# First group's gate stage: SP issues the stores of combined weights between and behind the two halves of a step's second block of weights

## The chip, the cores and the metric

The kernel runs on one core of a Trainium2 chip. The metric is the device time of one execution in microseconds (us), the median of three runs.

## The reference

A two-layer decoder trunk over 2048 tokens of width 1024, all in float32. The first layer is a chunked gated MLP: RMS norm with adaLN shift and scale, one projection to `u`, `v` and `z` of width 2048 each, a layer norm of `v`, a causal mixing of 128 positions by a 128x128 matrix for each of 8 channel groups, and an output projection:

```
u, v, z = jnp.split(h @ w_in, 3, axis=-1)
u = jax.nn.gelu(u)
v = layer_norm(jax.nn.gelu(v), ln_g, ln_b)
mixed = jnp.einsum("gts,bnsgc->bntgc", ws, vc) + b_s.T[:, :, None]
y = u * mixed.reshape(B, S, A_WIDTH) * jax.nn.silu(z)
return y @ w_out
```

The second layer is sliding-window attention with a shared rotary K/V, and a final RMS norm follows. The change touches only how the first layer is scheduled.

## The kernel before

**Precision and units.** Every float32 weight is used as two parts, a rounded one and the rest: ACT copies `w_raw` to `w_hi` (rounding, L1364), POOL forms `w_lo` = `w_raw` - `w_hi` (L1130), and PE does three matmuls for each product (L2361 to L2363). PE's work is cut into units. A unit's weights are one block of 128x4x512, in two halves of 128x2x512 that are loaded, rounded and subtracted one by one.

**Groups, stages, steps.** The first layer runs over four groups of 512 tokens. In each group come first the `v` units, then the gate stage, then the output projection. The gate stage has eight steps, one for each channel group g. A step has a first block of weights (buffer `w_raw0`) and a second block (buffer `w_raw1`), 48 matmuls of 128x512 each, and then 16 small mixing matmuls (L2566, with `w_s`). PE takes the first block half by half, so that a half's buffer is free after half of the block; the second block's pieces alternate between the halves, so that both halves are free only when the block is done, that is when the mixing starts, and both are needed at the next second block's start.

**Combined weights.** Groups 2 to 4 compute `v` and the output projection with fewer products, out of sums and differences of weight blocks. Those combinations are made once, during the first group's gate stage, from weights loaded for it. The list `COMBS` has 16: eight for the output projection ("a" in the list, output combinations below) and eight for `v` ("v", V combinations). For one of them SP loads 1 MB into a place `cbr` (`load_comb`, L858), DVE forms it by three differences (L1946 128x1024, L1948 and L1950 128x512), ACT rounds it to `cbh` (L1388), POOL forms the rest `cbl` (L1149: one operation for an output combination, two for a V one), and SP stores it (`keep_comb`: an output one by three DMAs of 512 KB, L866 twice and L869; a V one by two of 1 MB, L866). There are four places; a load into a place waits until the place's last combination is stored (the wait stands in front of L858). Weights of the second layer are split in the same stage (`split`: ACT L1378, POOL L1140, stores L843 and L844).

**What sets the order.** Every engine's order is written out by hand. SP issues all of these DMAs from one queue, in program order, and stands still at each wait. Its program for a step is `a_stage(i, q)` with q = g + 4: it loads the two blocks of step g when their buffers come free, stores what `load_comb` fetched two stages earlier, and loads new combinations. For the first group, most stages have one output and one V combination; q = 11 stores two V combinations; q = 10 and 12 also store a split. POOL's order in a step is: rests of the first block, rests of the second, split, output combination, V combination. DVE's is: the gate's products for a group (L2071, L2074, L2078, L2084), then the two combinations.

Of the kernel before, what the change touches and what calls it, by code (L numbers as in the profile page):

```python
# [20 lines left out]
GROUPS = 8  # L21
# [23 lines left out]
FIRST_B = FIRST[NG]  # L45
# [15 lines left out]
def group_of(u):  # L61
    return max(i for i in range(NG) if FIRST[i] <= u)
# [6 lines left out]
def uz_unit(i, g, ku):  # L69
    return FIRST[i] + V_UNITS[i] + 2 * g + ku  # L70
# [34 lines left out]
def kept_split(u):  # L105

    return of_blocks(u) and factor_of(u)[0] == "T" and not kept_whole(u)
# [41 lines left out]
def pieces_in(u):  # L149
    return 4 if of_blocks(u) else 8  # L150
# [37 lines left out]
def buffers():  # L188


    taken, before, last, turn = [], [], {}, [0, 1]
    for u in range(UNITS):
        i = group_of(u) if u < FIRST_B else NG
        if product_of(u) is not None and (u - FIRST[i]) % 3 == 2:
            b = 2
        elif out_product_of(u) is not None and u - ao_first(i) >= 4 and (u - ao_first(i)) % 3 == 1:
            b = 2
        elif out_product_of(u) is not None and u - ao_first(i) == 1:
            b = 3
        else:  # L200
            b = turn.pop(0)
            turn.append(b)
        taken.append(b)
        before.append(last.get(b))
        last[b] = u
    return taken, before


BUFFER, BEFORE = buffers()


def by_halves(u):

    if of_blocks(u):
        return True
    if u < FIRST_B:
        return u % 2 == 0
    kind, g, n, ku = B_UNITS[u - FIRST_B]
    return kind == "kv" or ku == 0 or (kind == "b" and n == 1 and g < NG - 1) or (kind == "qz" and n == 3 and g == 0)


def freed(u, hh):

    half = pieces_in(u) // 2
    return half + half * hh if by_halves(u) else 2 * half
# [31 lines left out]
def combs_at(i, q):  # L257
    return [c for c, comb in enumerate(COMBS) if comb[0] == i and comb[1] == q]
# [136 lines left out]
def yoco_kernel(nc, x, c, positions, a_norm, a_ada_w, a_ada_b, a_w_in, a_ln_g, a_ln_b, a_w_s, a_b_s,  # L395
# [3 lines left out]
    with ctx:  # L399
# [176 lines left out]
        def sem(name, per_group=0):  # L576
            s = ctx.enter_context(nc.semaphore(name))
            per[name] = per_group
            return s
# [22 lines left out]
        piece_done, kv_full = sem("piece_done"), sem("kv_full", 1)  # L602
# [51 lines left out]
        def pieces(u, k):  # L654

            return PIECES_BY[u] + k
# [120 lines left out]
        def _(sp):  # L777
# [6 lines left out]
            def a_half(u, hh):  # L784
                p, i = BUFFER[u], group_of(u)
                n = u - FIRST[i]
                there = raw[p][:, 2 * hh:2 * hh + 2]
                if kept_split(u):
                    if product_of(u) is not None:
                        kept = cbd[product_of(u)[0], factor_of(u)[1], hh]  # L790
                    else:
                        kept = cad[factor_of(u)[1], out_product_of(u)[1], hh]
                    for part, w in ((0, whi[p]), (1, wlo[p])):
                        sp.dma_start(w[:, 2 * hh:2 * hh + 2].bitcast(F32), kept[part]) \
                            .then_inc(raw_in[2 * p + hh], 16)
                elif kept_whole(u):
                    sp.dma_start(there, cad[factor_of(u)[1], out_product_of(u)[1], hh, 0]) \
                        .then_inc(raw_in[2 * p + hh], 16)
                elif out_product_of(u) is not None:
                    (_, odd, cols_half), pair = factor_of(u), 4 * out_product_of(u)[1] + 2 * hh  # L800
                    sp.dma_start(there, wo2[:, pair:pair + 2, odd, 512 * cols_half:512 * cols_half + 512]) \
                        .then_inc(raw_in[2 * p + hh], 16)
                elif product_of(u) is not None:
                    sv, m = product_of(u)
                    _, rows_half, cols_half = FACTORS[m]
                    kt, col = 4 * rows_half + 2 * hh, WIDTH + 1024 * sv + 512 * cols_half
                    sp.dma_start(there, wa[:, kt:kt + 2, col:col + 512]).then_inc(raw_in[2 * p + hh], 16)
                elif n < V_UNITS[i]:
                    j, kt = n // 2, 4 * (n % 2) + 2 * hh
                    sp.dma_start(there, wa[:, kt:kt + 2, WIDTH + 512 * j:WIDTH + 512 * j + 512]) \  # L810
                        .then_inc(raw_in[2 * p + hh], 16)
                else:
                    g, kt = (u - uz_unit(i, 0, 0)) // 2, 4 * (n % 2) + 2 * hh
                    sp.dma_start(there[:, :, 0:GD], wa[:, kt:kt + 2, GD * g:GD * g + GD]) \
                        .then_inc(raw_in[2 * p + hh], 16)
                    sp.dma_start(there[:, :, GD:2 * GD], wa[:, kt:kt + 2, 2 * WIDTH + GD * g:2 * WIDTH + GD * g + GD]) \
                        .then_inc(raw_in[2 * p + hh], 16)

            def b_half(u, hh):
                p = BUFFER[u]  # L820
                for m, w in ((0, whi[p]), (1, wlo[p])):
                    sp.dma_start(w[:, 2 * hh:2 * hh + 2].bitcast(F32), wsd[split_of(u, hh), m]) \
                        .then_inc(raw_in[2 * p + hh], 16)
# [16 lines left out]
            def keep_split(s):  # L840
                sp.wait_ge(split_lo, s + 1)
                m = SPLIT_SLOT[s]
                sp.dma_start(wsd[s, 0], wsh[m][:].bitcast(F32)).then_inc(split_out[m], 16)  # L843
                sp.dma_start(wsd[s, 1], wsl[m][:].bitcast(F32)).then_inc(split_out[m], 16)  # L844
# [16 lines left out]
            def keep_comb(c):  # L861
                _, _, whose, n, m = COMBS[c]
                sp.wait_ge(comb_lo, c + 1)
                to, some = (cad[:, n // 4] if whose == "a" else cbd[n // 4]), rounded_combs(c)
                for part, w in ((0, cbh[m]), (1, cbl[m])):
                    sp.dma_start(to[some, n % 4 // 2, part, :, n % 2].rearrange("t p n -> p t n"),  # L866
                                 w[:, some].bitcast(F32)).then_inc(comb_out[m], 16)
                if whose == "a":
                    sp.dma_start(to[1:4:2, n % 4 // 2, 0, :, n % 2].rearrange("t p n -> p t n"), cbr[m][:, 1:4:2]) \  # L869
                        .then_inc(comb_out[m], 16)  # L870
# [5 lines left out]
            def a_stage(i, q):  # L876

                first = uz_unit(i, 0, 0) - 8
                if i == 0 and q == 12:

                    sp.wait_ge(comb_out[0], combs_out(0, 0))
                    sp.wait_ge(comb_out[1], comb_out_before(len(COMBS) - 1))
                if q >= 1:
                    unit(first + 2 * q)
                if q == GROUPS + 4:
                    unit(first + 2 * q + 1)
                s = split_at(i, q - 2)
                if s is not None:
                    keep_split(s)
                for c in combs_at(i, q - 2):  # L890
                    keep_comb(c)
                if 1 <= q < GROUPS + 4:
                    unit(first + 2 * q + 1)
                if i == 0 and q < 4:
                    for n in range(KT * (2 + q), KT * (3 + q)):
                        load_ada(n)
                for c in combs_at(i, q):
                    load_comb(c)
                s = split_at(i, q)
                if s is not None:  # L900
                    if i == 0:
                        sp.wait_ge(ada_used, 6 * KT)
                    load_split(s)

            def unit(u):
                if BUFFER[u] == 2:

                    sp.wait_ge(y_done, at("y_done", group_of(u) - (product_of(u) is not None), 8))
                elif BUFFER[u] == 3:

                    i = group_of(u)
                    sp.wait_ge(piece_done, PIECES_BY[uz_unit(i, 0, 0)])
                    sp.wait_ge(comb_out[0], combs_out(0, 0))
                for hh in range(2):
                    if BEFORE[u] is not None:
                        sp.wait_ge(piece_done, pieces(BEFORE[u], freed(BEFORE[u], hh)))
                    if u < FIRST_B:
                        a_half(u, hh)
                    else:
                        b_half(u, hh)  # L920

            def load_x(n):
                if n >= 1:
# [106 lines left out]
            for s, slot in enumerate(SLOTS):  # L1030
# [9 lines left out]
                for k, pc in enumerate(slot):  # L1040
                    u = FIRST_B + pc // 8
# [4 lines left out]
                    kind, ug, n, ku, q = unit_of(pc)  # L1046
# [18 lines left out]
                    kind, ug, n, ku, q = unit_of(pc - 5)  # L1065
# [1713 lines left out]
```

## Time and profile before

| | |
|---|---|
| median of 3 runs | 2218.93 us (2217.34 to 2219.06) |
| profiled execution, its own time | 2219.44 us |
| its span | 2217.7 us |
| busy: PE, DVE, ACT, POOL | 97%, 65%, 49%, 54% |
| DMA packets of SP's queue | 73.5% of 16 engines' span |
| first group's gate stage, from the first mixing to the last | 158.55 to 336.72 us |

The share of busy time is over the whole span. Where PE's next matmul starts late, the view of waits names the engine that it waited for. Register, semaphore and DMA-issuing instructions are not counted as busy; an operation that is held up after it has started is counted as busy for all that time.

### The profile page before, as it was taken

Reading aid. Unit: us, or ns where it says so; the run is one execution under the profiler, and the core shown is the slowest. Engines: PE = TensorE matmul, PEld = TensorE weight load, DVE = VectorE, ACT = ScalarE, POOL = GpSimd, SP = SyncE. Lnnn points to the kernel's source line nnn. Section 1 sums busy time; section 2 is a strip of 40 time slices with the busy share of each in tenths; the row PEclk is TensorE's granted clock in tenths of the full one; section 3 lists DMA queues with packets and bytes.
Section 4 is the critical chain, followed back from the end, with each engine's and each line's share of the span. In section 5 each row is a group of like instructions: output and inputs, shape, how many; then the busy total and the mean of one; then the engine's idle time right before and its main releaser. Section 6 shows DMA issues by size and latency. Waiting matters only on the chain.

```text
span 2217.7 us, 29383 instructions
## 1 busy us (share of the span) xinstructions
PE 2150.9 (97%) x10410; PEld 1801.0 (81%) x10410; DVE 1440.5 (65%) x1761; ACT 1095.3 (49%) x2050; POOL 1195.1 (54%) x913
## 2 busy tenths in 40 slices
PE   5999999999999999999999999999999999999998
PEld 4887778788888878888777888887888888888887
DVE  6956548757486864554974673767767657656854
ACT  4334446634545744445653445534545646545653
POOL 3456675845553865544594645441535555454542
PEclk9999999999999999999999999999999999999999
DMA  9888889785558785557877556899686697887654
GB/s 347 307 306 308 312 315 356 231 308 174 196 198 324 285 315 191 200 179 269 314 259 283 181 181 218 323 348 365 244 297 225 253 359 266 280 309 288 206 205 171
DMA packets 244787, 592.89 MB, mean 267 GB/s; under 512 B 20929, under 2 KB 96801, under 8 KB 244257
## 3 DMA queue, kind: packets, MB, share of 16 engines
q1 hardware_dynamic: 241680, 585.71, 73.5%
q10 hardware_dynamic: 2960, 5.30, 0.7%
q8 instruction: 83, 1.36, 0.2%
q14 instruction: 64, 0.52, 0.1%
HBM read 461.96 MB, written 119.54 MB: 262 GB/s over the span
## 4 chain that ended last, share of the span: by engine, by line
PE 75%; DMA 6%; POOL 6%; DVE 5%; ACT 3%; DVEq 2%; POOLq 1%; issue 1%; SPq 1%; ACTq 0%
PE ps L2361 22%; PE ps L2363 22%; PE ps L2362 22%; DMA w_raw<-in_a_w_in 3%; POOL w_lo L1130 3%; PE ps L2566 2%; PE ps L2615 1%; PE ps L2616 1%; POOL cbl L1149 1%; PE ps L2641 1%; DVE acc L1812 1%; ACT w_hi L1364 1%; DMA w_lo<-a_weights_combined 1%; PE ps L2650 1%; DVE yb L2093 1%
## 5 line engine op out<-in xcount | busy, mean ns | idle before, releaser
L1130 POOL TENSOR_TENSOR w_lo<-w_raw,w_hi 128x1024 fp32r<-128x1024 f32 x244 | 650.0, 2682 | 569.6 <-ACT w_hi L1364 569.4
L1364 ACT ACTIVATE w_hi<-w_raw 128x1024 fp32r<-128x1024 f32 x260 | 272.0, 1057 | 418.3 <-DMA w_raw<-in_a_w_in 372.7
L2361 PE MATMUL ps<-h,w_hi 128*128 128x512 f32 x1024 | 403.3, 394 | 9.7 <-POOL w_lo L1130 8.3
L2363 PE MATMUL ps<-h,w_lo 128*128 128x512 f32 x1024 | 398.9, 390 | 0.0
L2362 PE MATMUL ps<-h,w_hi 128*128 128x512 f32 x1024 | 398.7, 389 | 0.0
L2361 PEld LDWEIGHTS ps<-h,w_hi 128*128 128x128 f32 x1024 | 192.2, 188 | 55.3 <-POOL w_lo L1130 14.3
L2363 PEld LDWEIGHTS ps<-h,w_lo 128*128 128x128 f32 x1024 | 192.2, 188 | 40.7
L2362 PEld LDWEIGHTS ps<-h,w_hi 128*128 128x128 f32 x1024 | 192.4, 188 | 38.9 <-issue 0.2
L2361 PE MATMUL ps<-r,w_hi 128*128 128x512 f32 x480 | 191.6, 399 | 1.9 <-issue 1.9
L2363 PE MATMUL ps<-r,w_lo 128*128 128x512 f32 x480 | 187.7, 391 | 0.0
L2362 PE MATMUL ps<-r,w_hi 128*128 128x512 f32 x480 | 187.3, 390 | 0.0
L2361 PE MATMUL ps<-w_hi,yb 128*128 128x512 f32 x448 | 179.2, 400 | 7.1 <-DVE w_lo L2116 3.5
L2071 DVE SCALAR_TENSOR_TENSOR wz<-wz,ps 128x512 f32<-128x512 f32 x64 | 43.7, 686 | 210.5 <-ACT wz L1580 210.5
L2363 PE MATMUL ps<-w_hi,yb 128*128 128x512 f32 x448 | 175.8, 392 | 0.0
L2362 PE MATMUL ps<-w_lo,yb 128*128 128x512 f32 x448 | 175.6, 392 | 0.0
L2093 DVE TENSOR_TENSOR yb<-vy,yb 128x1024 fp32r<-128x1024 f32 x48 | 114.4, 2383 | 42.5 <-ACT yb L1540 39.2
L1269 POOL TENSOR_SCALAR_AFFINE_SELECT p_edge<-pt 64x256 fp32r<-64x256 f32 x64 | 27.1, 423 | 187.7 <-ACT pt L1735 186.5
L2361 PE MATMUL ps<-w_hi,r 128*128 128x512 f32 (+1 forms) x352 | 125.5, 357 | 2.7 <-DMA r<-kv_input 1.7
L1735 ACT ACTIVATE pt<-ps 128x512 fp32r<-128x512 f32 x64 | 38.4, 600 | 179.6 <-PE ps L2641 179.2
L2363 PE MATMUL ps<-w_hi,r 128*128 128x512 f32 (+1 forms) x352 | 123.6, 351 | 0.0
L2362 PE MATMUL ps<-w_lo,r 128*128 128x512 f32 (+1 forms) x352 | 123.5, 351 | 0.0
L2361 PE MATMUL ps<-w_hi,h 128*128 128x512 f32 x272 | 107.9, 397 | 4.5 <-POOL w_lo L1130 4.2
(277 smaller groups left out, 4902.6 us busy)
## 6 DMA issues: line engine op xcount, KB each, us to landing
w_raw<-in_a_w_in SPq DMA_DIRECT2D x256, 256.0 KB, 3.6
w_hi<-b_weights_split SPq DMA_DIRECT2D x104, 512.0 KB, 4.7
w_lo<-b_weights_split SPq DMA_DIRECT2D x104, 512.0 KB, 6.3
w_raw<-in_a_w_in SPq DMA_DIRECT2D x52, 512.0 KB, 4.7
w_raw<-in_a_w_out SPq DMA_DIRECT2D x48, 512.0 KB, 5.4
w_hi<-v_weights_combined SPq DMA_DIRECT2D x48, 512.0 KB, 3.9
w_lo<-v_weights_combined SPq DMA_DIRECT2D x48, 512.0 KB, 5.2
w_hi<-a_weights_combined SPq DMA_DIRECT2D x32, 512.0 KB, 6.6
```

The source lines that it names most:

```text
L1130: g.tensor_tensor(wlo[p][:, rows_], raw[p][:, rows_], whi[p][:, rows_].bitcast(F32), ALU.subtract).then_inc(w_lo, 1)
L1149: last = g.tensor_tensor(cbl[m][:, rows_], cbr[m][:, rows_], cbh[m][:, rows_].bitcast(F32), ALU.subtract)
L1269: return g.affine_select(out=heads, in_=in_, compare_op=ALU.is_ge, fill=0.0, base=0, pattern=[[0, 4], [1, HEAD]], channel_multiplier=-1)
L1364: s_.activation(whi[p][:, rows_], raw[p][:, rows_], ACT.Copy).then_inc(w_hi, 1)
L1735: s_.activation(pt[:, 0, :], bank(6), ACT.Copy).then_inc(pt_hi, 1)
L1812: v.scalar_tensor_tensor(there, rows_, sc[:, kt:kt + 1], there, ALU.mult, ALU.add).then_inc(ada_used, 1)
L2071: v.scalar_tensor_tensor(wz[:, ft, :], wz[:, ft, :], 1.0, bank(2 + ft), ALU.add, ALU.mult) \
L2093: v.tensor_tensor(there[:, :, 1, :], y_factor(m, q), there[:, :, 0, :].bitcast(F32), ALU.subtract) \
L2361: t_.matmul(dst_, stat[0], mov[0], start=start, stop=False)
L2362: t_.matmul(dst_, stat[0], mov[1], start=False, stop=False)
L2363: return t_.matmul(dst_, stat[1], mov[0], start=False, stop=stop)
L2566: last = t_.matmul(bank(4 + ft, P, P * cnk), vs[:, cnk, P * ft:P * ft + P], wst[:, g, :], start=True, stop=True)
```

## The change

In the first group's gate stage, for q from 4 to 11, the loads and stores of a step's second block are interleaved: load the first half when it is free, store the first kept combination, load the second half, store the other combinations, store the split. Before, all stores came ahead of both halves. Other groups, and q = 12, keep their order. `unit_half` is cut out of `unit` and does what its loop did.

```diff
                 s = split_at(i, q - 2)
-                if s is not None:
+                if s is not None and (i >= 1 or q == GROUPS + 4):
                     keep_split(s)
-                for c in combs_at(i, q - 2):
-                    keep_comb(c)
-                if 1 <= q < GROUPS + 4:
-                    unit(first + 2 * q + 1)
+                kept = combs_at(i, q - 2)
+                if q == GROUPS + 4:
+                    for c in kept:
+                        keep_comb(c)
+                elif i == 0 and q >= 4:
+                    unit_half(first + 2 * q + 1, 0)
+                    if kept:
+                        keep_comb(kept[0])
+                    unit_half(first + 2 * q + 1, 1)
+                    for c in kept[1:]:
+                        keep_comb(c)
+                    if s is not None:
+                        keep_split(s)
+                else:
+                    for c in kept:
+                        keep_comb(c)
+                    if q >= 1:
+                        unit(first + 2 * q + 1)
...
+            def unit_half(u, hh):
+                if BEFORE[u] is not None:
+                    sp.wait_ge(piece_done, pieces(BEFORE[u], freed(BEFORE[u], hh)))
+                if u < FIRST_B:
+                    a_half(u, hh)
+                else:
+                    b_half(u, hh)
```

SP's queue at q = 6, before (`w_raw_50` is the second block's buffer; each half is one load of `u` columns, L814, and one of `z` columns, L816; cbh_104, cbl_100 and cbr_96 are the output combination, cbh_105 and cbl_101 the V one):

```order
L866 DMA a_weights_combined<-cbh_104 128x2x512
L866 DMA a_weights_combined<-cbl_100 128x2x512
L869 DMA a_weights_combined<-cbr_96 128x2x512
L866 DMA v_weights_combined<-cbh_105 128x4x512
L866 DMA v_weights_combined<-cbl_101 128x4x512
L814 DMA w_raw_50<-in_a_w_in 128x2x256
L816 DMA w_raw_50<-in_a_w_in 128x2x256
L814 DMA w_raw_50<-in_a_w_in 128x2x256
L816 DMA w_raw_50<-in_a_w_in 128x2x256
L858 DMA cbr_96<-in_a_w_out 128x1024 x2
L858 DMA cbr_97<-in_a_w_in 128x1024 x2
```

And after the change, at the same place:

```order
L814 DMA w_raw_50<-in_a_w_in 128x2x256
L816 DMA w_raw_50<-in_a_w_in 128x2x256
L866 DMA a_weights_combined<-cbh_104 128x2x512
L866 DMA a_weights_combined<-cbl_100 128x2x512
L869 DMA a_weights_combined<-cbr_96 128x2x512
L814 DMA w_raw_50<-in_a_w_in 128x2x256
L816 DMA w_raw_50<-in_a_w_in 128x2x256
L866 DMA v_weights_combined<-cbh_105 128x4x512
L866 DMA v_weights_combined<-cbl_101 128x4x512
L858 DMA cbr_96<-in_a_w_out 128x1024 x2
L858 DMA cbr_97<-in_a_w_in 128x1024 x2
```

The first half has moved ahead of five stores, the second ahead of two; the load into the V combination's place (cbr_97) now follows directly on the store from that place.

POOL's order for the same stretch, which is the same before and after (w_lo_57 belongs to first blocks, w_lo_58 to second blocks):

```order
L1130 TENSOR_TENSOR w_lo_57<-w_raw_49,w_hi_53 128x1024 x2
L1130 TENSOR_TENSOR w_lo_58<-w_raw_50,w_hi_54 128x1024 x2
L1149 TENSOR_TENSOR cbl_99<-cbr_95,cbh_103 128x2x512
L1149 TENSOR_TENSOR cbl_102<-cbr_98,cbh_106 128x1024 x2
L1130 TENSOR_TENSOR w_lo_57<-w_raw_49,w_hi_53 128x1024 x2
```

Nothing moves here: the rests of the next first block stand behind those of the V combination.

## Rows read from the trace of the kernel before

**Rows 1.** The page, parts 1 and 2: busy time by engine, granted clock.
```profile
PE 2150.9 (97%) x10410; PEld 1801.0 (81%) x10410; DVE 1440.5 (65%) x1761; ACT 1095.3 (49%) x2050; POOL 1195.1 (54%) x913
PEclk9999999999999999999999999999999999999999
```

**Rows 2.** Waits from 158 to 337 us: total us, times, longest.
```profile
ACT w_hi L1364 <- DMA w_raw<-in_a_w_in: 61.6, 17, 10.0
...
PE ps L2361 <- POOL w_lo L1130: 8.3, 9, 1.2
```

**Rows 3.** Windows cut at mixings: length, busy us (instructions), clock, DMA share, GB/s.
```profile
158.55:182.11 23.56, 23.56 (x113) 19.80 (x112) 16.04 (x11) 9.88 (x12) 12.86 (x5) 1.00 0.70 246
158.55:336.72 178.17, 169.32 (x785) 138.10 (x784) 100.03 (x83) 78.89 (x99) 125.58 (x49) 1.00 0.87 305
```

**Rows 4.** Timeline of PE: start, us, instruction, wait and releaser in brackets.
```profile
160.25 0.48 PE L2361 MATMUL ps<-h,w_hi 128*128 128x512 f32 x1
185.13 0.50 PE L2361 MATMUL ps<-h,w_hi 128*128 128x512 f32 x1 [1.07 <-POOL w_lo L1130]
199.18 0.50 PE L2361 MATMUL ps<-h,w_hi 128*128 128x512 f32 x1 [1.11 <-POOL w_lo L1130]
235.57 0.50 PE L2361 MATMUL ps<-h,w_hi 128*128 128x512 f32 x1 [0.87 <-POOL w_lo L1130]
312.92 0.50 PE L2361 MATMUL ps<-h,w_hi 128*128 128x512 f32 x1
```

**Rows 5.** Timeline of SP's queue at 182 us.
```profile
182.79 0.36 SPq L866 DMA_DIRECT2D v_weights_combined<-cbh  x1
183.75 1.10 SPq L814 DMA_DIRECT2D w_raw<-in_a_w_in  x1
```

**Rows 6.** Waits of SP's queue from 130 to 400 us.
```profile
SPq L866 <- POOL cbl L1149: 54.4, 14, 6.7
...
SPq L858 <- DMA v_weights_combined<-cbl: 2.9, 4, 1.0
```

**Rows 7.** Timeline of POOL, operation by operation.
```profile
217.00 2.71 POOL L1130 TENSOR_TENSOR w_lo<-w_raw,w_hi 128x1024 fp32r<-128x1024 f32 x1 [6.12 <-ACT w_hi L1364]
219.66 3.38 POOL L1130 TENSOR_TENSOR w_lo<-w_raw,w_hi 128x1024 fp32r<-128x1024 f32 x1
223.01 2.85 POOL L1149 TENSOR_TENSOR cbl<-cbr,cbh 128x1024 fp32r<-128x1024 f32 x1
228.43 4.77 POOL L1149 TENSOR_TENSOR cbl<-cbr,cbh 128x1024 fp32r<-128x1024 f32 x2 [2.58 <-ACT cbh L1388]
275.25 2.41 POOL L1140 TENSOR_TENSOR wsl<-wsr,wsh 128x1024 fp32r<-128x1024 f32 x1
```

**Rows 8.** Timeline of DVE.
```profile
189.43 1.21 DVE L1946 TENSOR_TENSOR cbr<-cbr 128x1024 f32<-128x1024 f32 x1
216.75 0.69 DVE L1950 TENSOR_TENSOR cbr<-cbr 128x512 f32<-128x512 f32 x1
217.36 3.43 DVE L1946 TENSOR_TENSOR cbr<-cbr 128x1024 f32<-128x1024 f32 x1
220.86 2.73 DVE L1948 TENSOR_TENSOR cbr<-cbr 128x512 f32<-128x512 f32 x1
```

**Rows 9.** L816 from 159 to 159.5 us: one load, issued to an idle queue.
```profile
DMA to landing us min/median/max: 3.1/3.1/3.1
```

**Rows 10.** DMA issues from 185 to 310 us: count, KB each, median us to landing.
```profile
w_raw<-in_a_w_in SPq DMA_DIRECT2D x39, 256.0 KB, 6.9
...
v_weights_combined<-cbl SPq DMA_DIRECT2D x5, 1024.0 KB, 7.7
...
a_weights_combined<-cbr SPq DMA_DIRECT2D x4, 512.0 KB, 4.8
```

**Rows 11.** Timeline of ACT.
```profile
192.39 1.06 ACT L1364 ACTIVATE w_hi<-w_raw 128x1024 fp32r<-128x1024 f32 x1 [8.67 <-DMA w_raw<-in_a_w_in]
226.43 1.92 ACT L1388 ACTIVATE cbh<-cbr 128x2048 fp32r<-128x2048 f32 x1 [7.09 <-DVE cbr L1950]
```

More of the change, by code:

```diff
@@ L914, in unit @@
                 for hh in range(2):
[L915 to L920, printed above, removed]
+                    unit_half(u, hh)
+            def unit_half(u, hh):
[5 more added lines that the diff above has]
+                    b_half(u, hh)
             def load_x(n):
```

## Prediction

> **What bounds the kernel now.** I read the page first. TensorE (PE) is busy 97% of the span, and the granted clock stands at 9 tenths or more in all 40 slices, so a change can only remove time in which PE waits [rows 1]. The change touches the first group's gate stage alone, so the second view is the list of waits cut to that stage: PE waited there 9 times, 8.3 us together, always for the `w_lo` that POOL makes. ACT in turn waited 61.6 us for weights from DRAM [rows 2].
>
> The third view cuts the stage at the mixing matmuls, which close a step. A step in which PE never waited takes 23.56 us; the seven steps take 178.17 [rows 3]. Seven times 23.56 is 164.92, so 13.25 us is the most that any reordering can win here, 0.6% of the time.
>
> The fourth view, PE's own rows, says where it waits. After the mixing at 182.11 the first block of the next step starts at 185.13, 1.07 us late; inside that step the second half of the second block starts at 199.18, 1.11 us late. Of the nine waits, two (1.07 and 0.87) stand before a first block and seven, 6.4 us, inside a step before a half of the second block [rows 4]. The first blocks of five successive steps start between 185.13 and 312.92: 127.8 us, 25.56 a step.
>
> Then SP's queue. The second block's buffer comes free when the mixing starts (182.11), but SP is then still held by the store of a V combination: it issues that at 182.79 and the first load of the second block only at 183.75 [rows 5]. In and around the stage SP waited 54.4 us in 14 waits for combinations to be rounded [rows 6].
>
> Last the views of POOL, DVE and ACT. They matter most. A difference on DVE over 128x512 takes 0.69 us when POOL is idle and 2.73 when a POOL subtraction runs: it ends at 223.59, 0.55 after POOL's operation (219.66 + 3.38 = 223.04). POOL's next one then ends at 225.86, 2.27 after DVE's. The two engines take turns, operation by operation [rows 7, 8].
>
> **What the change does, step by step.** No instruction is added or removed; on PE, DVE, ACT and POOL the order is the same. On SP, in steps q = 4 to 11 of the first group, the two loads of the second block's first half now stand ahead of the stores of the first kept combination (three for an output one, two for a V one), the second half's behind them, then the other combination's stores. A split's two stores go last.
>
> *Gain.* The first half is issued some 0.1 us after its buffer is free instead of 1.6 in the step at 182, and no longer behind a V combination's store of two times 1024 KB. A load issued to an idle queue landed in 3.1 us [rows 9]; those of this stage took 6.9 in the median [rows 10]. So the first half lands some 3.6 us after the mixing starts, where in the step at 182 ACT came to it 10.3 us after, at 192.39 [rows 11]. The second half has the three stores of an output combination ahead of it. The third of them would be issued 2 us after the mixing starts and landed 4.8 later before [rows 10]; with a microsecond for the half ahead that is 7.8, and the second half lands at about 9. PE needs the first half's rest 12.7 us after the mixing starts (1.7 of mixing to 160.25, then half of the 21.86 to 182.11) and the second's one piece (1.4) later, so the seven waits of 6.4 us should go, with the small restarts beside them.
>
> *Loss.* What becomes of the time is decided by the turns of POOL and DVE. Before, POOL sat idle waiting for the second block, 6.1 us ahead of 217.00 [rows 7], and DVE worked on its combinations meanwhile alone. After, POOL goes straight from the first block to the second, and each DVE operation waits for one of POOL's. I follow one step from the end of POOL's rest for a first block's first half, when PE starts that block, to the same point of the next step. In turns, a POOL operation costs 2.25 us (220.79 to 223.04), a DVE one over 1024 columns 1.1 (219.66 to 220.79) and one over 512 columns 0.55; alone DVE needs 1.2 and 0.7 [rows 7, 8]. In order: L2074 1.1, first block's second half 2.25, L2084 1.1, second block's first half 2.25, L1946 1.1, second block's second half 2.25, L1948 0.55, L1950 0.7, the V combination's L1946 1.2 (ACT rounds the output one meanwhile), POOL's output rest 2.25, L1948 0.55, L1950 0.75, ACT's rounding of the V combination 1.95 with its gap [rows 11], POOL's two rests of it 4.77, next first half 2.35, about half of that [rows 7]. With 0.15 of gaps: 25.3 us. Neither PE nor a transfer is in that loop, and it exceeds PE's 23.56.
>
> *Sum.* The first step is as before: its first half's load goes out at the same time as before, and by the same turns the V combination is formed at about 176 us either way. So PE starts its next block at 185.1. Then three steps of 25.3; the step with a split adds a POOL operation of 2.3 (2.41 alone [rows 7]): 27.6; the step with two V combinations has 3.3 + 6.75 + 1.25 + 1.95 + 9.55 + 2.35 = 25.2. Together 128.7, against 127.8: 0.9 us lost, PE's last first block at 313.8. In the last step no output combination is left; before, it took 23.80 from 312.92 to the mixing at 336.72 [rows 3, 4]; without waits it takes 21.86 (160.25 to 182.11): 1.9 won. Its second half is due 12.3 us after the block starts (10.9 and 1.4). Behind a V combination's store it lands some 11 us after the mixing, 7.5 after the block's start; with ACT's 1.1, POOL's 2.3 and a turn it is there at about 12. Sum: 1.0 us less.
>
> *Covered edits.* The output stores now go out up to 8 us later; the next load into that place (L858) comes a step's queue later and has nearly a step before DVE reads it. The split's stores moved last cost 0.8 us of issue; the load behind it waits for them, with the other transfers as cover. Were that cover gone, it is the last rival.
>
> A rule of the Trainium skill speaks against the change: SBUF — State Buffer, section "SBUF: two separate sides", says that DVE with two SBUF operands and GpSimd hold a shared port pair exclusively for a whole instruction, the loser blocking. The trace agrees: 0.69 against 2.73 us [rows 8]. By it, the sum is the one above; if they shared bandwidth instead, POOL's earlier start would not delay DVE so, and the 6.4 us would largely stay won.
>
> The sum is made against the profiled execution: 2219.44 - 1.0 = 2218.4. That execution lies 0.5 over the median of the runs, 2218.93, so the forecast is 2218.
>
> **Rivals.** *The waits go and don't come back.* If DVE's operations fall into POOL's gaps better than my order of turns (a second half that comes late lets DVE finish first), steps cost 24 to 24.9 and the gain is 3 to 8 on the five steps plus 1.9; the second block's waits alone give 6.4, which puts the time at 2212.5; all 13.25 would give 2205.7. For it: POOL's own work is 125.58 of 178.17 us [rows 3]. Against it: in turns, seven POOL operations (16.1) and eight of DVE (some 7.1) already fill 23.2 us a step, and ACT's 1.95 stands in series.
>
> *The first block's loads come late.* SP now stands at L858 until the V store that it has just issued lands; before, that cost 2.9 us in 4 waits, since the loads stood between [rows 6]. Worked on from above, the second half lands 9 us after the mixing starts, and the V store, issued behind it with its second part landing 7.7 us after issue [rows 10], at 14 to 17; the combination's load and the next first block's follow at 6.9 from issue, so that its halves land at 21 to 25, where before the first of them could be issued from 7.2 on, when PE is through half of the first block. The transfers' busy share is already 0.87 over the stage [rows 3]. POOL's loop asks for the first half rounded at 25 to 26.5, so landed by about 24. From there each microsecond costs one in each of five steps: 2 us late makes 10, 2228.
>
> **How the numbers follow.** Forecast 0.58, its own range 2215 to 2221 (half a microsecond of error in each of six steps); the faster rival 0.25; the slower 0.17. A measurement of this kernel tells about 0.2%, 4.4 us, from no change. The faster rival passes that bound in most of its cases (0.20) and the forecast rarely (0.02); the slower one in 0.14, the forecast 0.02. So faster 0.22, same 0.62, slower 0.16. The range runs from 2210.5, which keeps most of the faster rival, to 2223.5, a loss of one microsecond in five steps, leaving about one in ten out on either side.
>
> **What would show it.** Right: the waits for `w_lo` inside a step gone, larger ones (1 to 2 us) in front of first blocks; POOL without its 6 us pauses; more DVE operations at L1946 to L1950 of 2.7 to 3.4 us; PE's first blocks some 25.3 us apart. Wrong to the fast side: first blocks 23.6 to 24.5 apart. Wrong to the slow side: ACT waiting for first-block loads, with SP's longest waits at L858. My order of turns fails if DVE runs several operations in a row while POOL has work ready.

## The result, and the profile after

The changed kernel takes 2225.61 us in the median of 8 runs (2219.82 to 2229.42), the kernel before 2218.06 in as many beside it: a ratio of 1.0029, 95% interval 1.0020 to 1.0039, some 6.4 us slower. The forecast was 2218 us, no change, with a range up to 2223.5.

The profiled execution took 2226.81 us. On the page the engines are as busy as before [rows 1]; only DVE's busy time has grown, by 10.8 us, with the same 1761 instructions, since an operation that POOL holds up counts as busy.

```profile
PE 2152.4 (97%) x10410; PEld 1803.4 (81%) x10410; DVE 1451.3 (65%) x1761; ACT 1093.1 (49%) x2050; POOL 1194.9 (54%) x913
```

To find the place I cut both traces at three points: where PE starts the first block behind the first mixing, where it starts the output projection (behind the last mixing), and where it ends the first mixing of the second group. The view is that of windows: length, busy us with instructions, granted clock, DMA share, GB/s. Before:

```profile
160.25:338.43 178.18, 169.33 (x788) 138.11 (x786) 100.05 (x84) 79.80 (x101) 125.58 (x49) 1.00 0.88 309
338.43:522.83 184.40, 181.48 (x819) 148.53 (x818) 124.89 (x132) 97.51 (x127) 119.45 (x57) 1.00 0.79 281
522.83:2217.70 1694.87, 1664.45 (x8178) 1401.60 (x8176) 1101.83 (x1427) 857.16 (x1744) 876.78 (x753) 1.00 0.72 257
```

After, cut at the same three points (its first row also answers to [rows 3]):

```profile
162.00:342.36 180.36, 170.15 (x788) 141.24 (x786) 113.49 (x84) 79.83 (x100) 128.04 (x49) 0.98 0.90 307
342.36:531.80 189.44, 182.23 (x819) 148.31 (x818) 129.00 (x132) 97.22 (x127) 117.03 (x57) 1.00 0.78 279
531.80:2225.10 1693.30, 1662.08 (x8178) 1399.11 (x8176) 1095.02 (x1427) 855.30 (x1744) 876.66 (x753) 1.00 0.71 257
```

The seven steps lost 2.2 us, and the way from the output projection to the second group, in which the change moves nothing, lost 5.0. The rest gives 1.6 back and the start had lost 1.8 before the gate stage began; both lie outside the change and vary as much among the kernels below (the start is at 160.1 to 162.4, the rest at 1690.6 to 1697.8). So it is the two stretches that I compare from here on.

PE's timeline, which answers to [rows 4]: the start of each first block, and one second half.

```profile
162.00 0.48 PE L2378 MATMUL ps<-h,w_hi 128*128 128x512 f32 x1
186.70 0.50 PE L2378 MATMUL ps<-h,w_hi 128*128 128x512 f32 x1 [0.85 <-POOL w_lo L1147]
212.05 0.50 PE L2378 MATMUL ps<-h,w_hi 128*128 128x512 f32 x1 [1.51 <-POOL w_lo L1147]
237.50 0.50 PE L2378 MATMUL ps<-h,w_hi 128*128 128x512 f32 x1 [1.60 <-POOL w_lo L1147]
264.52 0.50 PE L2378 MATMUL ps<-h,w_hi 128*128 128x512 f32 x1 [3.19 <-POOL w_lo L1147]
292.16 0.71 PE L2378 MATMUL ps<-h,w_hi 128*128 128x512 f32 x1 [2.19 <-POOL w_lo L1147]
317.81 0.50 PE L2378 MATMUL ps<-h,w_hi 128*128 128x512 f32 x1 [0.23 <-POOL w_lo L1147]
331.00 0.50 PE L2378 MATMUL ps<-h,w_hi 128*128 128x512 f32 x1 [0.65 <-POOL w_lo L1147]
```

The steps last 24.70, 25.35, 25.45, 27.02, 27.64, 25.65 and, up to 342.36, 24.55 us. Inside the steps one wait of 0.65 is left where there were seven of 6.4 together; the waits stand in front of the first blocks, as the forecast had it. The fourth step is too long for its loop of turns. SP's waits from 130 to 400 us, which answer to [rows 6], say why:

```profile
SPq L858 <- DMA v_weights_combined<-cbl: 26.6, 4, 7.2
...
SPq L866 <- POOL cbl L1166: 3.9, 1, 3.9
```

SP hardly waits for combinations to be rounded any more (54.4 us before). It stands at L858 instead, until the V store that it has just issued has landed: 26.6 us in 4 waits, against 2.9 (the same line's waits for output stores grew from 0.7 to 9.6). In the fourth step SP's timeline, beside [rows 5], reads:

```profile
241.27 0.60 SPq L866 DMA_DIRECT2D v_weights_combined<-cbl  x1
...
251.72 0.80 SPq L858 DMA_DIRECT2D cbr<-in_a_w_in  x2
...
253.05 0.51 SPq L814 DMA_DIRECT2D w_raw<-in_a_w_in  x1
```

The view of that V store gives its landing, 10.4 us after the issue at 241.27, which is 251.7:

```profile
DMA to landing us min/median/max: 10.4/10.4/10.4
```

The next first block's load is issued only at 253.05, and POOL, which had ended the V combination's rests at 260.56 (255.84 + 4.72), waits for ACT and ACT for that load:

```profile
255.84 4.72 POOL L1166 TENSOR_TENSOR cbl<-cbr,cbh 128x1024 fp32r<-128x1024 f32 x2 [3.34 <-ACT cbh L1405]
260.99 1.06 ACT L1381 ACTIVATE w_hi<-w_raw 128x1024 fp32r<-128x1024 f32 x1 [3.27 <-DMA w_raw<-in_a_w_in]
262.12 2.35 POOL L1147 TENSOR_TENSOR w_lo<-w_raw,w_hi 128x1024 fp32r<-128x1024 f32 x1 [1.56 <-ACT w_hi L1381]
```

Those 1.56 us are what the fourth step lasts beyond the third. PE then goes on with the output projection, where it waited 1.2 us before, and now 6.3. Three of its rows:

```profile
354.95 0.47 PE L2378 MATMUL ps<-w_hi,yb 128*128 128x512 f32 x1 [1.45 <-DMA w_lo<-a_weights_combined]
362.40 0.47 PE L2378 MATMUL ps<-w_hi,yb 128*128 128x512 f32 x1 [1.74 <-POOL w_lo L1147]
374.94 0.47 PE L2378 MATMUL ps<-w_hi,yb 128*128 128x512 f32 x1 [1.41 <-DVE w_lo L2133]
```

The first names a transfer, and so does ACT's row for the raw block that SP loads just behind the projection's start; below it stands ACT's row of before:

```profile
358.76 1.06 ACT L1381 ACTIVATE w_hi<-w_raw 128x1024 fp32r<-128x1024 f32 x1 [6.10 <-DMA w_raw<-in_a_w_out]
```

```profile
349.76 1.06 ACT L1364 ACTIVATE w_hi<-w_raw 128x1024 fp32r<-128x1024 f32 x1 [1.03 <-DMA w_raw<-in_a_w_out]
```

Counted from the start of the projection (342.36 and 338.43) that is 16.4 us against 11.3. SP issued the load as early as before, 3.0 us after the projection's start in both (345.37 and 341.44), but it landed after 13.4 us instead of 8.3. The queue was full. DMA's share (the last figure but one; 1.00 and a little over is full) around q = 11, first in two stretches of the kernel after, then in two of the kernel before:

```profile
312.36:317.36 5.00, 5.00 (x32) 4.42 (x30) 0.46 (x1) 4.07 (x6) 5.00 (x3) 1.00 0.21 63
317.36:362.36 45.00, 40.98 (x186) 33.11 (x185) 24.88 (x21) 19.18 (x22) 23.94 (x11) 1.00 1.04 373
```

```profile
303.43:308.43 5.00, 5.00 (x24) 4.14 (x23) 0.00 (x0) 3.10 (x6) 5.00 (x4) 1.00 0.34 124
334.00:336.00 2.00, 2.00 (x10) 1.68 (x9) 2.00 (x1) 0.60 (x1) 1.06 (x1) 1.00 0.05 18
```

Before, the two V stores of q = 11 (twice 1 MB each) went out at 305.88 and 310.58, the first 7.0 us ahead of the block at 312.92, and the transfers had run out of work once more at 334 to 336, just ahead of the projection. After, the transfers idle from 313 to 317, while the first V store, ready since about 310 by POOL's rows, stands behind a half that is not free yet; it goes out at 316.75, the second at 320.51, and then the share stays at 1.04 until 362.

### The profile page after: what moved, and what is told of

Read it like the earlier page. It is cut to its first block, busy times and chain, and to the rows that moved or that the text cites. A ratio compares the mean times of both kernels' runs of the same rounds, so it can differ in the third digit from the quotient of the medians.

```text
span 2225.1 us, 29383 instructions
## 1 busy us (share of the span) xinstructions
PE 2152.4 (97%) x10410; PEld 1803.4 (81%) x10410; DVE 1451.3 (65%) x1761; ACT 1093.1 (49%) x2050; POOL 1194.9 (54%) x913
## 4 chain that ended last, share of the span: by engine, by line
PE 73%; DVE 7%; DMA 6%; POOL 5%; ACT 3%; DVEq 2%; issue 1%; POOLq 1%; SPq 1%; ACTq 0%
PE ps L2378 22%; PE ps L2380 21%; PE ps L2379 21%; POOL w_lo L1147 3%; PE ps L2583 2%; DMA w_raw<-a_weights_combined 1%; DVE yb L2110 1%; PE ps L2632 1%; PE ps L2633 1%; DMA w_raw<-in_a_w_in 1%; PE ps L2658 1%; DMA v_weights_combined<-cbl 1%; DVEq L1964 1%; DVE acc L1829 1%; POOL cbl L1166 1%
## 5 line engine op out<-in xcount | busy, mean ns | idle before, releaser
L2378 PE MATMUL ps<-h,w_hi 128*128 128x512 f32 x1024 | 403.5, 394 | 11.4 <-POOL w_lo L1147 10.2
L2378 PEld LDWEIGHTS ps<-w_hi,yb 128*128 128x128 f32 x448 | 84.1, 188 | 35.1 <-issue 12.9
```

What stands on the lines that cost most here:

```text
L2378: t_.matmul(dst_, stat[0], mov[0], start=start, stop=False)
```

## Experiments

**Theories.** Theory 1: the 5 us of the output projection come from q = 11 alone, whose two V stores now leave too late and fill the queue ahead of the projection's loads; the gate steps lose for another reason, SP's stand at L858. Theory 2: everything comes from the steps q = 4 to 10, by POOL's and DVE's turns and by late stores that pile up over many steps. "Theories" in the expectations are these; steps are counted there by q where the number is over seven.

The table has, for each kernel's profiled execution, the seven steps and the way from the projection's start to the end of the second group's first mixing, cut as above, what they are together against before (362.58 us), and the measured ratio to before where it was timed.

| kernel | seven steps | way to group 2 | together | ratio (95%) |
|---|---|---|---|---|
| before | 178.18 | 184.40 | | |
| after | 180.36 | 189.44 | +7.2 | 1.0029 (1.0020 to 1.0039) |
| e1, q = 11 alone | 176.92 | 189.38 | +3.7 | 1.0009 (0.9999 to 1.0018) |
| e2, q = 4 to 10 alone | 182.91 | 183.80 | +4.1 | 1.0023 (1.0014 to 1.0032) |
| e3, first store ahead | 177.40 | 184.52 | -0.7 | 1.0007 (0.9996 to 1.0019) |
| e4, after, short rests | 181.24 | 186.73 | +5.4 | one run |
| e5, before, short rests | 166.80 | 184.69 | -11.1 | one run |
| e6, first block first | 175.07 | 188.15 | +0.6 | 1.0007 (0.9997 to 1.0017) |
| e7, last store only | 175.88 | 185.45 | -1.3 | 1.0000 (0.9990 to 1.0011) |
| e8, e6 and e7 | 177.44 | 186.02 | +0.9 | 1.0010 (1.0001 to 1.0019) |

Each sum (0.1% is 2.2 us) lies inside its interval, so the two stretches can account for the times; each sum is of a single execution, and the start and the rest vary by more than some of them.

### e1: the new order in q = 11 alone

`GROUPS` is 8, so `GROUPS + 3` is q = 11.

```diff
-                if s is not None and (i >= 1 or q == GROUPS + 4):
+                if s is not None and (i >= 1 or q != GROUPS + 3):
...
-                elif i == 0 and q >= 4:
+                elif i == 0 and q == GROUPS + 3:
```

> The new order in step 11 alone, the steps 4 to 10 as before. If the loss of the changed kernel is the backlog that step 11's held-back V stores leave for the output projection (theory 1), the loop of gate steps runs as before, within 1 us of its 178.2 us, and the output projection is 4 to 6 us longer than its 93.2 us: 2221 to 2224 us. If the loss comes from the steps before (turns of POOL and DVE at 25.3 us, first block's loads late in steps 8 and 9; theory 2), this run is no slower than before: 2216 to 2219 us, with the output projection at 93 to 94 us.

The windows of the seven steps and of the output projection proper (to the first matmul behind it; 93.15 us before), and then two around the V stores:

```profile
160.08:337.00 176.92, 168.86 (x788) 138.27 (x786) 100.70 (x84) 79.53 (x100) 124.70 (x49) 1.00 0.87 304
337.00:435.86 98.86, 92.67 (x419) 74.67 (x418) 76.85 (x59) 59.56 (x75) 63.51 (x28) 1.00 0.84 299
...
302.00:312.00 10.00, 10.00 (x53) 8.52 (x52) 1.35 (x2) 5.39 (x9) 10.00 (x5) 1.00 0.02 6
312.00:357.00 45.00, 41.25 (x190) 33.45 (x188) 25.02 (x21) 19.31 (x22) 24.13 (x11) 1.00 1.04 372
```

The projection is 5.7 us longer, as long as in the changed kernel (98.94), with q = 4 to 10 untouched. Ten microseconds of idle transfers (0.02), then 45 of full ones (1.04): the same stores, late. The gate steps won 1.3, in the last one (24.39 against 25.51). Theory 1 holds for the projection. The time, 2220.03 us (ratio +2.0 us, -0.2 to +4.0), is a little under the expected 2221 to 2224.

### e2: the new order in q = 4 to 10, the old one in q = 11

```diff
-                if s is not None and (i >= 1 or q == GROUPS + 4):
+                if s is not None and (i >= 1 or q >= GROUPS + 3):
...
-                elif i == 0 and q >= 4:
+                elif i == 0 and 4 <= q < GROUPS + 3:
```

> The new order in the steps 4 to 10, step 11 in the old one. Theory 1: the output projection is back at 93 to 94 us, the gate steps keep the changed kernel's lateness of some 2 us (180 us), with perhaps 1 us more, as the last step waits for its stores again: 2219 to 2221 us. Theory 2: the output projection is still some 5 us longer, as the backlog is that of all steps: 2223 to 2226 us.

The projection is back at 93.18 us, as theory 1 has it. But the gate steps lost 4.7 us, not 2 to 3, and with 2223.65 us the time is what theory 2 gave. Fourth and fifth step repeat the changed kernel's (26.62, 27.65), and SP stands at L858 for 27.0 us in 4 waits. The last step takes 27.50: it now has a wait of 2.63 inside, since both V stores stand ahead of its second block again, as before the change, and the first block's loads ahead of them went out later (11.0 and 9.9 us ahead of the block's start, and 20.0 and 14.6 before). That is read from SP's rows and not tested by itself. So q = 4 to 10 cost by themselves, and q = 11 costs elsewhere: neither theory covers both.

### e3: the first kept combination ahead of both halves

```diff
                 elif i == 0 and q >= 4:
-                    unit_half(first + 2 * q + 1, 0)
                     if kept:
                         keep_comb(kept[0])
+                    unit_half(first + 2 * q + 1, 0)
                     unit_half(first + 2 * q + 1, 1)
```

> The first kept combination stays ahead of both halves, as before the change; the other stores still go out behind both halves. Theory 1: the early stores use the DMA's idle time ahead of the mixing, only one combination is left behind it, and the backlog at the output projection is at most a third of the changed kernel's: a projection of 93 to 95 us, gate steps of 25.3 us, 2216 to 2220 us. Theory 2 (every store moved behind a half delays what follows): the projection stays 4 us or more longer, 2222 to 2226 us.

Both losses are gone, and only the split's step is long: steps of 24.88, 25.33, 25.31, 25.30, 27.31, 25.64 and 23.63, and a projection of 93.99. SP stands at L858 as long as in the changed kernel (27.9 us in 4 waits), but it comes there earlier: in the fourth step it issues the V store at 237.17 instead of 241.27 and is free at 247.40, 9.5 us after the block's start and not 14.2. The stand costs only where it ends too late. The time, 2220.86 us, is 0.9 over the expected range and can't be told from before.

### e4: the changed kernel with short rests

```diff
-                        last = g.tensor_tensor(cbl[m][:, rows_], cbr[m][:, rows_], cbh[m][:, rows_].bitcast(F32),
-                                               ALU.subtract)
+                        last = g.tensor_tensor(cbr[m][:, rows_, 0:8], cbr[m][:, rows_, 0:8],
+                                               cbh[m][:, rows_, 0:8].bitcast(F32), ALU.subtract)
...
-                for part, w in ((0, cbh[m]), (1, cbl[m])):
+                for part, w in ((0, cbh[m]), (1, cbr[m])):
```

> The changed kernel, but GpSimd makes the rest of the combined weights for 8 of 512 columns only, so that the rests of the combined weights are left out. If the turns of POOL and DVE cap the gate steps at 25.3 us, as the prediction had it, the steps fall to the 23.6 us of a step that waits for nothing, where the DMA allows: 166 to 172 us for seven steps, not 180. If transfers cap them, the steps stay at 25 us or more and the seven at 178 us or more. The lateness of the output projection's loads stays as in the changed kernel (theory 1: they are behind stores of unchanged size).

A miss: POOL is busy 79 us of the steps instead of 128, and they take 181.24 us. Only the first fell to 23.64; then come 26.28, 25.18, 28.16, 26.33, 26.43 and 25.22. What holds the fourth one is on SP, ACT and POOL:

```profile
242.84 0.67 SPq L866 DMA_DIRECT2D v_weights_combined<-cbr  x1
...
253.15 0.80 SPq L858 DMA_DIRECT2D cbr<-in_a_w_in  x2
...
254.47 0.51 SPq L814 DMA_DIRECT2D w_raw<-in_a_w_in  x1
...
262.00 1.06 ACT L1381 ACTIVATE w_hi<-w_raw 128x1024 fp32r<-128x1024 f32 x1 [6.56 <-DMA w_raw<-in_a_w_in]
...
263.13 2.34 POOL L1147 TENSOR_TENSOR w_lo<-w_raw,w_hi 128x1024 fp32r<-128x1024 f32 x1 [9.18 <-ACT w_hi L1381]
```

POOL had nothing to do for 9.18 us; the first block's load had waited for the V store to land. So the changed order has a second loop: mixing, second block, V store, its landing, the next first block's load, ACT, POOL, PE. Not all of the 181.24 us is that loop's:

```profile
162.27:343.51 181.24, 172.43 (x788) 142.79 (x786) 96.95 (x84) 79.83 (x101) 79.18 (x49) 0.96 0.91 311
```

The granted clock fell behind three waits in front of first blocks (2.43, 3.67 and 1.80 us), and the steps that followed them, the third, fifth and seventh, took 25.18, 26.33 and 25.22 us without a wait at their end: there PE's own slower pace set the time. Whether the turns mattered at all was open; hence the next run.

### e5: the kernel before with short rests

The edit of e4 on the kernel before.

> The kernel before with GpSimd's rests of the combined weights made for 8 of 512 columns only (they are left out), the counterpart of the run with the changed order. If the turns of POOL and DVE cap the steps of the kernel before (my forecast's loop), the seven steps fall from 178 us towards 7 x 23.6 = 165 us: 165 to 170 us; the changed order's 181 us with the same short rests is then a loop of its own, over SP's stand at L858 for the V store's landing. If the transfers cap the steps in either order, they stay at 175 to 180 us here too.

```profile
161.51:328.31 166.80, 165.21 (x788) 138.56 (x786) 100.54 (x84) 79.51 (x101) 79.83 (x49) 1.00 0.93 329
161.51:185.07 23.56, 23.56 (x116) 19.81 (x114) 14.56 (x13) 11.00 (x14) 11.39 (x7) 1.00 0.92 328
```

Six of the seven steps take 23.56 us (23.55 to 23.57), as long as PE's work without a wait; one takes 25.44. So POOL's rests of the combined weights are what makes the steps of the kernel before longer than PE's work, and the transfers carry 23.56 us a step at a share of 0.93. That it is the turns with DVE is not shown by this run: SP's waits for those rests, ahead of the second block's loads (54.4 us [rows 6]), are gone with them. With the rests out of the way the new order costs 14.4 us against the old one (181.24 against 166.80). Half of that, 7.2 us, is PE's busy time (172.43 against 165.21), stretched by the fallen clock; the other half is PE's waiting.

### e6: the next step's first block ahead of the new combinations

```diff
                 if q >= 1:
                     unit(first + 2 * q)
+                if i == 0 and q >= 5:
+                    load_parts(i, q - 1)
...
+                if i >= 1 or q < 4:
+                    load_parts(i, q)
+
+            def load_parts(i, q):
                 for c in combs_at(i, q):
                     load_comb(c)
```

> The changed kernel, but from step 5 on the loads of the combinations to come (and of the split) are issued behind the next step's first block, so that SP does not stand for the V store's landing ahead of that block. If that stand is what made steps 4 and 5 of the stage (27.0 and 27.6 us) long, the first becomes 25.3 to 25.5 us, the second stays at 27.3 to 27.6 us (POOL's turn with the split's rest): seven steps in 178 to 179 us. The output projection stays 5 us longer (189 us to the second group's first mixing): 2222 to 2225 us. If the stand is not the cause, the fourth step stays at 27 us. If loads that come later hurt the combinations, DVE waits for them and the steps grow past 26 us.

SP's waits at L858 fall from 26.6 to 2.6 us, and the fourth step from 27.02 to 25.16: the stand was the cause, together with the combinations' loads that SP issued between it and the first block's, since the edit moves both. The projection stayed late (188.15). But the fifth step, expected at 27.3 to 27.6 for POOL's turn with the split, took 25.34. In e8, which has the same order up to there, it took 27.34. The two traces part in that step. DVE's and POOL's rows, first e6, then e8:

```profile
269.12 0.69 DVE L1973 TENSOR_TENSOR cbr<-cbr 128x512 f32<-128x512 f32 x1
269.72 1.22 DVE L1969 TENSOR_TENSOR cbr<-cbr 128x1024 f32<-128x1024 f32 x1
...
269.93 3.27 POOL L1153 TENSOR_TENSOR w_lo<-w_raw,w_hi 128x1024 fp32r<-128x1024 f32 x1 [2.74 <-ACT w_hi L1387]
```

```profile
271.67 2.77 DVE L1977 TENSOR_TENSOR cbr<-cbr 128x512 f32<-128x512 f32 x1
...
271.48 2.41 POOL L1157 TENSOR_TENSOR w_lo<-w_raw,w_hi 128x1024 fp32r<-128x1024 f32 x1 [1.74 <-ACT w_hi L1391]
```

In e6 DVE began its last short difference (L1973) 0.81 us ahead of POOL's rest, took 0.69 for it, and got the next operation in too. In e8 POOL began 0.19 us ahead of DVE's, which took 2.77. DVE's difference began 8.57 and 8.56 us after the block's start; what differs is POOL's rest, at 9.38 and 8.37 us, since its half had landed a microsecond later in e6. By these rows, who comes first at one point makes 2.0 us of the step, and here the later load made the shorter step. I have one trace of each, so how often it falls which way is open.

### e7: of the change, only the last store moved

```diff
-                elif i == 0 and q >= 4:
-                    unit_half(first + 2 * q + 1, 0)
-                    if kept:
-                        keep_comb(kept[0])
-                    unit_half(first + 2 * q + 1, 1)
-                    for c in kept[1:]:
-                        keep_comb(c)
-                    if s is not None:
-                        keep_split(s)
+                elif i == 0 and q == GROUPS + 3:
+                    keep_comb(kept[0])
+                    unit(first + 2 * q + 1)
+                    keep_comb(kept[1])
```

The split's stores go out ahead of the combinations again, as before the change.

> Of the change only this is kept: in step 11 the second V store goes out behind the second block, the first V store stays ahead of it; the steps 4 to 10 are as before. If the backlog comes of holding back both V stores together (theory 1), the last step falls to 23.6 us as with the first combination ahead in all steps, the other steps stay at 25 to 25.9 us, and the way to the second group's first mixing stays at 184 to 185 us: 2216 to 2217.5 us. If any store behind the second block makes the backlog, that way is 187 us or more and the time 2219 to 2221 us.

The last step falls from 25.51 to 23.60 us, and the way to group 2 is 185.45 (184.40 before, 189.38 in e1): with the first V store out at 307.51, in the transfers' idle time, the second one alone makes no backlog to speak of. That is 1.3 us less in the two stretches; the medians, 2218.01 (expected at most 2217.5) against 2217.64, can't tell it from nothing.

### e8: e6 and e7 together

```diff
+                elif i == 0 and q == GROUPS + 3:
+                    keep_comb(kept[0])
+                    unit(first + 2 * q + 1)
+                    keep_comb(kept[1])
                 elif i == 0 and q >= 4:
                     unit_half(first + 2 * q + 1, 0)
```

on top of e6's edit.

> The changed order in the steps 4 to 10 with the loads of the combinations behind the next step's first block, and step 11 with its first V store ahead of the second block and its second behind it. If the two losses are the two that the runs so far name (SP's stand ahead of the first block, and both V stores of step 11 held back) and they add, the seven steps take 175 us as in the run with the loads behind the first block, and the way to the second group's first mixing 184 to 185.5 us: 2.5 to 3.5 us less than before in these two stretches, 2214 to 2216 us in all if what comes later is as before. If that way stays at 188 us, the held-back stores of the steps 4 to 10 make a backlog too, and the time is 2218 to 2219 us.

The projection's part came (186.02, half a microsecond over what was expected), the steps' part not: 177.44, with 2.0 us of the difference in the fifth step told under e6. At 2219.1 us, and not the expected 2214 to 2216, it is slower than before by 0.1 (0.01 to 0.19)%. No version that makes all the rests beats the kernel before.

## Why the prediction was wrong, step by step

**The waits inside the steps** went, as worked out: one of 0.65 us is left of seven.

**The loop of turns** was right where nothing else came in: 25.35 and 25.45 us against a forecast of 25.3. The forecast also said that no transfer is in that loop, and there the changed kernel is no proof of it: from 186.8 to 264.4 POOL waited 8.9 us in 4 waits for halves that ACT rounded as they landed. In e3 it did not, and its second to fourth steps took the forecast time, 25.33, 25.31 and 25.30 us. POOL's waits there, from 187.3 to 263.1:

```profile
POOL cbl L1166 <- ACT cbh L1405: 17.5, 6, 3.3
```

The split's step was forecast at 27.6 and took 27.64, 27.65, 27.31 and 27.34 in the four kernels after, e2, e3 and e8; e6's 25.34 shows that the order of turns is not fixed there. The Trainium skill (SBUF — State Buffer, "SBUF: two separate sides") says that whichever of the two engines starts first keeps the shared port pair for the whole instruction; the rows of e6 and e8 agree, with 0.69 us for the one that came first and 2.77 for the one that came 0.19 late.

**"Covered edits" is the step that failed.** It priced stores that leave later at nothing and left SP's stand behind them to a rival. In the fourth step the rival came true, at 1.6 us: the V store landed 10.4 us after its issue, not 7.7 (in e3, with the three output stores out long before, 10.2, so that what made it slow is open), and 17.8 us after the mixing at 233.95, where the rival had 14 to 17. And it looked at each store only from the side of its own place and step. It never asked what the stores of q = 11 meet when they land 9 and 12 us later, counted from the projection's start, the last of them only 7.4 us ahead of it: the output projection's first loads, in a queue that before had run dry just ahead of them. That is 5.0 us, the largest term of the result, and no line of the prediction has it. The rival on first blocks had the mechanism (the store delays loads behind it), but the larger loss lay in another place.

**The last step** was to win 1.9 us and won 1.0 (24.55 against 25.51; without waits 23.60 in e7). Its second half landed 11.8 us after the mixing at 315.63 (327.41), and I had some 11. What was sized wrong is the block's start, 2.2 us after that mixing and not 3.5, so that the half was due earlier and PE waited 0.65 us after all. In e6, with the same order of stores, the block started 3.7 us after the mixing, the half landed 12.0 after it, and the step took 23.60.

**The step with two V combinations** was forecast at 25.2 and took 25.65, with a wait of 0.23 behind it. In e6 it took 25.64 with a wait of 1.76, so the loop there is 0.4 us longer than forecast; why so little of the wait is left in the changed kernel is told below.

Together: the steps were forecast at 177.2 us (178.18 less 1.0) and took 180.36, the projection at no change and took 5.0 more. 3.2 and 5.0 make the 8.2 by which the two stretches missed.

The Trainium skill (DMA: Bandwidth & Descriptors, "Queues, rings and completion order") says that a DMA engine takes the descriptors of a ring in order. By that, a load issued behind a store waits for the store's bytes; the trace agrees, with 13.4 us instead of 8.3 for one load issued at the same point.

## What to carry to other kernels

Where one queue carries loads and stores, a store is not free because nobody waits for it: it takes the queue's time from whatever is issued next, so follow it past the end of the stage that issues it, and look for the stretch in which the transfers stand idle (a share of 0.05 from 334 to 336 us here, and 0.34 around the first V store), which is where it should go. Do not put a ready store behind a wait for something else. And when a wait for one thing is taken out of an engine's program, read what its next wait is for: SP exchanged 50 us of waiting for POOL, which held up one block, for 24 more of waiting for its own store, which held up another.

## What the runs showed of the hardware that was not expected

TensorE's clock fell inside the gate stage. The granted clock of the seven steps is 0.98 instead of 1.00, and windows of 2 us behind the two longest waits in front of first blocks (3.19 and 2.19 us) show where:

```profile
264.52:266.52 2.00, 2.00 (x6) 1.57 (x7) 1.52 (x3) 1.79 (x3) 2.00 (x1) 0.61 1.03 376
266.52:268.52 2.00, 2.00 (x7) 1.59 (x6) 1.92 (x2) 0.00 (x0) 2.00 (x2) 0.53 1.03 327
...
292.16:294.16 2.00, 2.00 (x5) 1.61 (x6) 1.91 (x3) 0.96 (x1) 2.00 (x1) 0.53 1.05 396
```

That is the level of 1.2 GHz for most of 4 us; a matmul there took 0.63 us instead of 0.39:

```profile
293.10 0.63 PE L2380 MATMUL ps<-h,w_lo 128*128 128x512 f32 x1
...
295.91 0.39 PE L2378 MATMUL ps<-h,w_hi 128*128 128x512 f32 x1
```

From 292.16 to 295.91 PE started 9 matmuls, one each 0.42 us, where its pace is 0.23: 1.7 us more of PE's work in that step, the one with two V combinations. The step was not longer for it. Here is that step of the changed kernel, and then of e6, whose clock stayed at 1.00 through it:

```profile
292.16:317.81 25.65, 25.42 (x113) 21.02 (x113) 14.37 (x12) 11.89 (x14) 21.51 (x9) 0.93 0.85 297
```

```profile
285.89:311.53 25.64, 23.88 (x112) 19.88 (x113) 16.59 (x13) 11.99 (x14) 21.44 (x9) 1.00 0.95 338
```

In e6 PE waited 1.76 us behind it, in the changed kernel 0.23: the slower pace took the place of a wait. The split's step shows the same, 27.64 us here against 27.31 and 27.34 at full clock in e3 and e8, 0.3 us at most. In e4, where PE waited for nothing behind such steps, the fallen clock did lengthen them.

In front of all first blocks stand the 16 small mixing matmuls and then the wait. Behind those of 1.51 and 1.60 us (212.05 and 237.50) the clock stayed at 1.00, as it did behind e6's 1.76 there and behind e2's 2.63 inside a step; behind e4's 1.80 in front of a first block it fell. So the length of the wait alone does not tell, and several waits of a microsecond shifted into one of two or three can bring the clock down.
